# GpSimd instead of VectorE makes the low parts of 14 weight tiles in the first block of a three-block layer kernel

## The chip, the core and the metric

The kernel runs on one core of a Trainium2 chip. The metric is the device time of one execution in microseconds (us). Three executions of the kernel before took 2788.99, 2790.64 and 2792.49 us; the median is 2790.64 us.

The engines are named as the profile names them: PE is TensorE, DVE is VectorE, ACT is ScalarE, POOL is GpSimd, SP is SyncE, which here issues the weight loads.

## The reference, cut to what matters

Three blocks follow each other on a sequence of 256 positions of width 1024, all in float32. The change lies in the middle of the first block, between its first feed-forward part and its memory attention:

```python
h = x @ w_in
g_ssd, g_att, z, xbc, dt_raw, q, c_kv, q_idx, k_idx, w_idx = split_cols(h, IN_SPLITS)
y_ssd = ssd_branch(z, xbc, dt_raw, ...)          # a scan over the sequence, then a gated norm
# dsa_branch: an index score picks 64 of 256 keys for each query, then attention over them
q_lat = einsum('bthd,hdr->bthr', q, w_uk)
score = where(causal, sum over heads of relu(q_idx @ k_idx) * w_idx, -inf)
_, idx = lax.top_k(score, topk)
y_att = softmax(q_lat @ c_kv[idx] - slope * dist) @ c_kv[idx], then @ w_uv
merged = sigmoid(g_ssd) * (y_ssd @ w_proj_ssd) + sigmoid(g_att) * (y_att @ w_proj_att)
x = layer_norm(ALPHA * x + merged @ w_out)
```

The kernel makes keys from `c_kv @ w_uk` and values from `c_kv @ w_uv` and does the attention as an ordinary masked one.

## The kernel before

Every matrix product is done with float32 precision from operands that TensorE takes in a reduced form (`fp32r`). A weight tile of up to 128 x 2048 elements is loaded into a buffer `raw`. ScalarE copies it, rounded, to `hi` (line 693); another engine then computes `lo = raw - hi` in place of `raw` (line 696). For each product TensorE issues three matmuls, lines 714 to 716: high by high, high by low, low by high.

The list `SEQ` fixes the order of all weight tiles. Outside the expert part of block two there are six `raw` buffers and three `hi` buffers, used in turn, so tile n can be rounded once TensorE has used tile n-3. `split_tile` is called for each tile by ScalarE (rounds) and by VectorE (subtracts), at the point of each engine's program that `refill` sets: after the step that belongs to tile n-3. For the tiles in the list `POOLED`, VectorE skips the call and GpSimd does the subtraction, at a place in GpSimd's program that is written out by hand. In the kernel before these are two tiles each of `misc`, `rva` and `sva` and the two tiles that follow the experts.

Each engine runs its instructions in order. A wait on a semaphore holds up everything that is queued behind it on that engine.

In the stage of the change (`tiles1`, with the side work of `pe_side1`, `act_side1`, `dve_side1` woven in, one side step after each tile) the tiles come in this order: `qi` 4, `ki` 1, `z` 4, `gs` 4, `q` 4, `uk` 1, `uv` 1, `ps` 4, `ga` 4; `pa` 4 follow. The 14 tiles from `q` to `ga` are the ones that the change moves. On VectorE the side work under these tiles is, in this order:

- the gated norm of the scan: line 1592, eight instructions in a row, `Yt = Yt * rs * nrow`, both tensors in SBUF;
- the index scores: line 1657 (`LG`, from PSUM), a reduction (line 1663), and the additions into `sc` (lines 1666 and 1669, both operands in SBUF);
- the search for the 64 largest (lines 1676, 1678), the mask made from it (line 1682 with one tensor operand, line 1684 with two in SBUF);
- eight attention steps: per step four times line 1704 (`bt` from `kd` and `MA`, both in SBUF), twice line 1707 (`SS` from PSUM and `bt`), the row maximum (line 1208), its negation (line 1210, 128x4), then of the step before the scaled output (line 1244, from PSUM) and the transposed scores (line 1234, from PSUM). Line 1608 drains the `ps` product from PSUM.

In the loop of `tiles1` VectorE does its part for a tile in the order: evictions, one side step, `refill` (the `lo` of the next tile), one more side step. GpSimd has nothing to do in this stage but to wait, after the loads of `drow`, `mraw`, `nrow` and `kd` at 213 to 215 us, for the start of the transposes of the attention's output (`o1`, 503 us), when it loads `mem` into the same buffer.

Of the kernel before, what the change touches and what calls it, by code (L numbers as in the profile page):

```python
# [79 lines left out]
def sequence():  # L80
    s = seq_ffn([("f1u", "f1d")], FF // P)
    s += seq_tm("misc", 8, 288, 288) + seq_fm("xbc", 8, 2048, 256)
    s += seq_fm("qi", 8, D, 256) + seq_fm("ki", 8, 128, 128) + seq_tm("z", 8, D, 512) + seq_tm("gs", 8, D, 512)
    s += seq_fm("q", 8, D, 256) + seq_fm("uk", 2, D, D) + seq_tm("uv", 2, D, D)
    s += seq_tm("ps", 8, D, 512) + seq_tm("ga", 8, D, 512) + seq_tm("pa", 8, D, D)
    s += seq_tm("mva", 8, 512, 512) + seq_tm("wo", 8, D, D)
    s += seq_fm("mk", 8, D, 256) + seq_fm("mq", 8, D, 256) + seq_tm("mvb", 8, 512, 512) + seq_tm("mo", 8, D, D)
    s += seq_ffn([("f2u", "f2d")], FF // P)
    s += seq_tm("rva", 8, 512, 512) + seq_fm("rqk", 8, 2048, 256) + seq_tm("rvb", 8, 1536, 512)
    s += seq_tm("rg", 8, 2048, 512)  # L90
    s += seq_tm("ro", 16, D, D)
    s += seq_ffn([("f3u", "f3d")], FF // P)
    s += seq_tm("sva", 8, 512, 512) + seq_fm("sk", 8, D, 256) + seq_fm("sq", 8, D, 256)
    s += seq_tm("svb", 8, 512, 512) + seq_tm("so", 8, D, D)
    s += seq_fm("rt", 8, P, P)
    s += seq_experts()
    for name in ("t1", "t2", "t4", "t5", "t3"):
        s += seq_tm(name, 8, 512, 512)
    s += seq_fm("gb", 8, P, P) + seq_fm("cf", 8, 512, 256)
    s += seq_tm("c1k", 16, 256, 256) + seq_tm("c1v", 16, 256, 256) + seq_tm("za", 8, 512, 512)  # L100
    s += seq_tm("gma", 8, D, 512) + seq_tm("ba", 4, D, 512) + seq_tm("zb", 8, 512, 512)
    s += seq_tm("gmb", 8, D, 512) + seq_tm("bb", 4, D, 512) + seq_tm("o3", 8, D, D)
    return s
# [144 lines left out]
SEQ = sequence()  # L248
OFFS = np.cumsum([0] + [P * nc_ * k for _, _, nc_, _, k in SEQ])
E0 = min(n for n, q in enumerate(SEQ) if q[0] == "e0u")  # L250
E1 = 1 + max(n for n, q in enumerate(SEQ) if q[0] == f"e{NE - 1}d")

POOLED = [n for name in ("misc", "rva", "sva") for n, q in enumerate(SEQ) if q[0] == name] + [E1, E1 + 1]
A1 = 2.0 ** 0.25
A2 = 4.0 ** 0.25

# [1 line left out]
def cells(n):  # L258
    return SEQ[n][2] * SEQ[n][4]
# [163 lines left out]
def program(nc, d, out):  # L423
    ctx = ExitStack()
    with ctx:
# [3 lines left out]
        def sb(c, name, shape, dt=F32):  # L429
            return c.take(name, shape, dt)  # L430
# [12 lines left out]
        def f32(ap):  # L443
            return ap.bitcast(F32)
# [63 lines left out]
        misc = sb(one_, "misc", [P, 2, 288])  # L508
# [160 lines left out]
        book, ps = Book(), {}  # L669
# [11 lines left out]
        def split_tile(L, n):  # L681

            if L.kind == "V" and n in POOLED:
                return
            slot, before, _ = HI_AT[L.path]
            m = cells(n)
            hi = HI[slot[n]][:, 0:m]
            raw, lo = [x[:, 0:m] for x in RAW[RAW_AT[L.path][0][n]]]
            if L.kind == "A":
                if before[n] is not None:  # L690
                    L.wait_ge("used", before[n])
                L.wait_ge("raw", n)
                L.e.activation(hi, raw, ACT.Copy).then_inc(*L.up("hi", n))  # L693
            else:
                L.wait_ge("hi", n)
                L.e.tensor_tensor(lo, raw, f32(hi), ALU.subtract).then_inc(*L.up("lo", n))  # L696
# [259 lines left out]
        def pool_gb(G, j, *after):  # L956
            for point in after:
                G.wait_ge(*point)
            src = d["rows"][j * 2 * D:(j + 1) * 2 * D].partition_broadcast(P)
            G.e.dma_start(GB[:, :, :].rearrange("p a n -> p (a n)"), src).then_inc(  # L960
                *G.landed(sem_ld["gb"], 16 * (j + 1), "lnw", j))

        def small_load(G, name, dst, src):
            G.e.dma_start(dst, src).then_inc(*G.landed(sem_ld[name], 16, name))

        def row_src(o, n):
            return d["rows"][o:o + n].partition_broadcast(P)
# [1234 lines left out]
        def met(L, name):  # L2202
            for kind in "TAV":
                L.wait_ge(name, kind)

        def branch(L, few, many):

            if L.kind in "TAV":
                meet(L, "moe")
            else:  # L2210
                met(L, "moe")
            v = L.e.value_load(flag[0:1, 0:1], min_val=0, max_val=1)
            seen, at = L.seen, L.next
            with L.e.If(v == 0):
                L.path, L.seen = "z", dict(seen)
                few(L)
            with L.e.Else():
                L.path, L.seen, L.next = "o", dict(seen), at
                many(L)
            L.path, L.seen = None, seen  # L2220
# [994 lines left out]
            run(ev_tm(V, "o3", 8, D, D, ev_o3))  # L3215

        def pool_end(G):
            for n in POOLED[6:8]:
                split_tile(G, n)
            G.wait_ge("norm", 7, 1)  # L3220
            G.wait_ge("scr")
            for tt in range(2):
                n = P * (tt + 1)
                src = bass.AP(d["scr"].tensor, T - 1 - tt * P, [[384, P], [P * 385, 16], [1, n]])
                small_load(G, f"bi{tt}", BI[:, :, tt * P:tt * P + n], src)
            small_load(G, "cm", cm_[:, :, :, :].rearrange("p a t c -> p (a t c)"), d["c_cmpm"])
            small_load(G, "w2", W2[:, :, :, :].rearrange("p a b n -> p (a b n)"), d["w2c"])
# [211 lines left out]
        def gpsimd(G):  # L3439
            G.wait_ge("raw", 0)  # L3440
            small_load(G, "cols", cols[:, :], d["cols"])
            pool_gb(G, 0, ("raw", 2))
            for n in POOLED[0:2]:
                split_tile(G, n)
            pool_gb(G, 1, ("norm", 0, 1))
            met(G, "f1")
            small_load(G, "drow", drow[:, :], row_src(16 * D, 48))
            small_load(G, "mraw", mraw[:, :], d["c_mneg4"])
            small_load(G, "nrow", nrow[:, :], row_src(16 * D + 48, D))
            small_load(G, "kd", kd[:, :, :, :].rearrange("p a t k -> p (a t k)"), d["c_dsa"])  # L3450
            G.wait_ge("o1", 6)
            small_load(G, "mem", M[:, :, :], d["mem"].rearrange("a (t p) n -> p (a t) n", p=P))
            pool_gb(G, 2, ("norm", 1, 1))
            pool_gb(G, 3, ("norm", 2, 1))
            for n in POOLED[2:4]:
                split_tile(G, n)
            pool_gb(G, 4, ("norm", 3, 1))
            met(G, "f2")
            small_load(G, "rope", rope[:, :, :].rearrange("p a t -> p (a t)"), d["c_rope"])
            small_load(G, "decay", DT[:, :, :, :].rearrange("p m h t -> p (m h t)"), d["c_decay"])  # L3460
            pool_gb(G, 5, ("norm", 4, 1))
            met(G, "ro")
            small_load(G, "hot", hot[:, :], d["c_hot"])
            small_load(G, "hneg", hneg[:, :], d["c_hneg"])
            small_load(G, "rel", rb[:, :], d["rel"])
            G.wait_ge("ev", ("dist",))
            src = dr[:, 0:384].unsqueeze(1).to_broadcast([16, P, 384])
            small_load(G, "scr", bass.AP(d["scr"].tensor, 0, [[P * 385, 16], [385, P], [1, 384]]), src)
            for n in POOLED[4:6]:
                split_tile(G, n)  # L3470
            pool_gb(G, 6, ("norm", 5, 1))
            met(G, "f3")
            small_load(G, "cs", cs[:, :, :].rearrange("p a n -> p (a n)"), d["c_sb"])
            pool_gb(G, 7, ("norm", 6, 1))
            met(G, "so")
            small_load(G, "nrow3", nrow3[:, :], row_src(17 * D + 48, D))
            branch(G, pool_end, pool_end)

        def sync(S):
# [3 lines left out]
            for n in range(E0 + RAWS):  # L3483
                load_tile(S, n)
            branch(S, sync_end, sync_end)

        kinds = (("T", "pe", tensor), ("A", "act", scalar), ("V", "dve", vector), ("G", "pool", gpsimd),
                 ("S", "sp", sync))
        sems = {k: {None: sem(f"s_{n}"), "z": sem(f"s_{n}_z"), "o": sem(f"s_{n}_o")} for k, n, _ in kinds}
# [44 lines left out]
```

## Time and profile before

| what | value |
| --- | --- |
| median of 3 executions | 2790.64 us |
| the profiled execution's own time | 2788.26 us |
| its span (first to last instruction) | 2786.1 us |
| PE busy in the span | 2639.0 us (95%) |
| DVE busy | 1946.9 us (70%) |
| ACT busy | 1528.6 us (55%) |
| POOL busy | 50.7 us (2%), 8 subtractions and DMA issues |
| line 696 on DVE, all of the kernel | 574 instructions, 1311.1 us |
| mean granted TensorE clock | 0.972 |

Times within the span are counted from its start. A row of the timeline gives the start, the time taken, engine, line, operation, output and inputs with their shapes, how many equal instructions were merged into it, and in brackets how long the engine had stood idle before it and what ended that. Most of the kernel is bound by TensorE; the stage from 365 to 505 us is one of the few in which TensorE stands idle several times.

### The profile page before, as it was taken

To read this page: it belongs to the slowest core of one execution; us is meant where nothing else is said; L and a number is where in the kernel's file an instruction comes from. 1 tells how busy PE (TensorE), PEld (TensorE's weight loads), DVE (VectorE), ACT (ScalarE), POOL (GpSimd) and SP (SyncE) were. 2 spreads that over 40 slices of the span, in tenths; PEclk is the share of its full clock that TensorE was granted. 3 is DMA by queue.
4 is the path that set the end of the run, shared out by engine and by line. 5 is a ranking of instruction groups with operands and counts; after the bars stand their busy time and mean duration, and the time that the engine had idled before them with its cause. 6 is when DMAs were issued, how large, how long until landed. Compare 5 with 4: busy or idle time off the path is not lost.

```text
span 2786.1 us, 34409 instructions
## 1 busy us (share of the span) xinstructions
PE 2639.0 (95%) x14799; PEld 2281.5 (82%) x14799; DVE 1946.9 (70%) x1940; ACT 1528.6 (55%) x1602; POOL 50.7 (2%) x38
## 2 busy tenths in 40 slices
PE   8999989998999998999878999999999999979998
PEld 7999877796998877998766888888888888867886
DVE  4457689565556665445547898988989898976854
ACT  4436445443444353434536777777777777755742
POOL 0000000000001000001000000000000000010000
PEclk9999999998999999999878999999999999989999
DMA  6545333452555534585227999999999999965332
GB/s 249 191 173 185 133 121 122 166 196 92 185 192 202 181 136 168 183 225 191 93 84 277 346 358 347 359 341 341 359 346 358 345 357 348 359 243 191 137 121 77
DMA packets 88640, 632.28 MB, mean 227 GB/s; under 512 B 9792, under 2 KB 9808, under 8 KB 13472
## 3 DMA queue, kind: packets, MB, share of 16 engines
q1 hardware_dynamic: 84496, 610.24, 59.7%
q0 software_dynamic: 3984, 19.76, 2.6%
q8 instruction: 118, 1.93, 0.3%
q14 instruction: 42, 0.34, 0.0%
HBM read 625.77 MB, written 4.19 MB: 226 GB/s over the span
## 4 chain that ended last, share of the span: by engine, by line
PE 85%; DVE 10%; ACT 3%; DMA 1%; issue 1%; DVEq 0%; POOL 0%; SPq 0%; ACTq 0%; POOLq 0%
PE pw L714 14%; PE pw L715 14%; PE pw L716 14%; PE py L714 12%; PE py L715 11%; PE py L716 11%; DVE lo L696 3%; ACT hi L693 1%; DMA raw<-in_wts 1%; PE pw L2404 1%; DVE XL L908 1%; PE pw L2341 1%; PE pw L870 1%; PE pw L2342 1%; PE pw L895 1%
## 5 line engine op out<-in xcount | busy, mean ns | idle before, releaser
L696 DVE TENSOR_TENSOR lo<-raw,hi 128x2048 fp32r<-128x2048 f32 x406 | 926.1, 2282 | 406.0 <-ACT hi L693 405.7
L693 ACT ACTIVATE hi<-raw 128x2048 fp32r<-128x2048 f32 x414 | 786.0, 1900 | 411.2 <-PE py L716 327.0
L714 PE MATMUL pw<-XH,hi 128*128 128x256 f32 x1688 | 484.0, 287 | 14.6 <-DVE lo L696 5.1
L715 PE MATMUL pw<-XL,hi 128*128 128x256 f32 x1688 | 481.9, 285 | 0.0
L716 PE MATMUL pw<-XH,lo 128*128 128x256 f32 x1688 | 481.7, 285 | 0.0
L696 DVE TENSOR_TENSOR lo<-raw,hix 128x2048 fp32r<-128x2048 f32 x168 | 385.0, 2292 | 53.5 <-ACT hix L693 49.6
L715 PE MATMUL pw<-lo,GH 128*128 128x512 f32 x896 | 354.2, 395 | 0.0
L714 PEld LDWEIGHTS pw<-XH,hi 128*128 128x128 f32 x1688 | 328.4, 195 | 19.9 <-DVE lo L696 6.1
L693 ACT ACTIVATE hix<-raw 128x2048 fp32r<-128x2048 f32 x168 | 321.7, 1916 | 39.2 <-PE py L716 37.6
L715 PEld LDWEIGHTS pw<-XL,hi 128*128 128x128 f32 x1688 | 328.4, 195 | 1.1
L716 PEld LDWEIGHTS pw<-XH,lo 128*128 128x128 f32 x1688 | 328.3, 194 | 0.0
L715 PE MATMUL py<-lo,hh 128*128 128x512 f32 x712 | 279.8, 393 | 0.0
L714 PE MATMUL py<-hi,XH 128*128 128x512 f32 (+1 forms) x480 | 195.5, 407 | 16.6 <-DVE XL L908 14.8
L715 PEld LDWEIGHTS pw<-lo,GH 128*128 128x128 f32 x896 | 169.3, 189 | 34.7
L714 PE MATMUL py<-hi,hh 128*128 128x512 f32 x484 | 190.7, 394 | 0.9 <-DVE hl L1110 0.5
L716 PE MATMUL py<-hi,XL 128*128 128x512 f32 (+1 forms) x480 | 190.2, 396 | 0.0
L715 PE MATMUL py<-lo,XH 128*128 128x512 f32 (+1 forms) x480 | 189.9, 396 | 0.0
L716 PE MATMUL py<-hi,hl 128*128 128x512 f32 x484 | 189.8, 392 | 0.0
L714 PE MATMUL pw<-hi,GH 128*128 128x512 f32 x452 | 184.5, 408 | 2.5 <-issue 2.5
L716 PE MATMUL pw<-hi,GL 128*128 128x512 f32 x452 | 179.7, 398 | 0.0
L714 PE MATMUL pw<-hix,GH 128*128 128x512 f32 x444 | 178.4, 402 | 0.0
L716 PE MATMUL pw<-hix,GL 128*128 128x512 f32 x444 | 174.6, 393 | 0.0
(509 smaller groups left out, 3840.0 us busy)
## 6 DMA issues: line engine op xcount, KB each, us to landing
raw<-in_wts SPq DMA_DIRECT2D x577, 1024.0 KB, 4.8
GB<-in_rows POOLq DMA_DIRECT2D x8, 1024.0 KB, 4.9
scratch_bias<-dr POOLq DMA_DIRECT2D x1, 3072.0 KB, 36.0
BI<-scratch_bias POOLq DMA_DIRECT2D x1, 2048.0 KB, 12.0
raw<-in_wts SPq DMA_DIRECT2D x3, 512.0 KB, 3.2
raw<-in_wts SPq DMA_DIRECT2D x2, 576.0 KB, 3.6
X<-in_x SPq DMA_DIRECT2D x1, 1024.0 KB, 5.4
nrow<-in_rows POOLq DMA_DIRECT2D x2, 512.0 KB, 4.6
```

The lines of the kernel that those rows point to most:

```text
L693: L.e.activation(hi, raw, ACT.Copy).then_inc(*L.up("hi", n))
L696: L.e.tensor_tensor(lo, raw, f32(hi), ALU.subtract).then_inc(*L.up("lo", n))
L714: T_.e.matmul(o, x[0], w[0], start=first, stop=False)
L715: T_.e.matmul(o, x[0], w[1], start=False, stop=False)
L716: return T_.e.matmul(o, x[1], w[0], start=False, stop=last)
L870: e = T_.e.transpose(o, src(tt, f0 + f), ident)
L895: e = T_.e.transpose(b[:, f * P:f * P + P], src[:, tt, (f0 + f) * P:(f0 + f + 1) * P], ident)
L908: V.e.tensor_tensor(lo[:, f0:f0 + 4, tt * P:tt * P + P], ps[key, tt, f0][:, :].rearrange("p (f t) -> p f t", f=4), f32(hi[:, f0:f0 + 4, tt ...
L2341: T_.e.matmul(b[:, f * P:f * P + P], TH[:, tt, fs], SL[:, tt, :], start=tt == 0, stop=False)
L2342: q = T_.e.matmul(b[:, f * P:f * P + P], TL[:, tt, fs], SL[:, tt, :], start=False, stop=tt == 1)
L2404: q = T_.e.transpose(bt_[:, g * P:g * P + P], ghf[(i - 1) % 2][:, g, :], ident)
```

## The change

`POOLED` gets the 14 tiles of `q`, `uk`, `uv`, `ps` and `ga`. So VectorE skips their subtraction, and GpSimd does all 14 in a row, after the load of `kd` and before it waits for `o1`. ScalarE's rounding, the loads, the buffers and TensorE's program stay as they are. The other edits only name the earlier pooled tiles in another way.

```diff
-POOLED = [n for name in ("misc", "rva", "sva") for n, q in enumerate(SEQ) if q[0] == name] + [E1, E1 + 1]
+def tiles_of(*names):
+    return [n for n, q in enumerate(SEQ) if q[0] in names]
+
+
+POOLED = tiles_of("misc", "q", "uk", "uv", "ps", "ga", "rva", "sva") + [E1, E1 + 1]
...
             small_load(G, "nrow", nrow[:, :], row_src(16 * D + 48, D))
             small_load(G, "kd", kd[:, :, :, :].rearrange("p a t k -> p (a t k)"), d["c_dsa"])
+            for n in tiles_of("q", "uk", "uv", "ps", "ga"):
+                split_tile(G, n)
             G.wait_ge("o1", 6)
             small_load(G, "mem", M[:, :, :], d["mem"].rearrange("a (t p) n -> p (a t) n", p=P))
```

Line numbers of the changed file are four higher here (696 is 700 there). GpSimd's program around the new place, before:

```order
L964 DMA kd<-in_c_dsa 128x1536
L964 DMA O<-in_mem 128x2x1024
L960 DMA GB<-in_rows 128x2048 x2
L696 TENSOR_TENSOR lo<-raw,hi 128x2048 x2
L960 DMA GB<-in_rows 128x2048
```

and after:

```order
L968 DMA kd<-in_c_dsa 128x1536
L700 TENSOR_TENSOR lo<-raw,hi 128x2048 x14
L968 DMA O<-in_mem 128x2x1024
L964 DMA GB<-in_rows 128x2048 x2
L700 TENSOR_TENSOR lo<-raw,hi 128x2048 x2
```

Fourteen subtractions now stand ahead of the load of `mem` into the buffer `O`.

VectorE's program at the index scores and the search for the largest, before (`sc` holds the scores, `m` the eight largest found):

```order
L854 COPY C<-pw 128x512
L1657 TENSOR_SCALAR LG<-pw,wi 128x256 x4
L1663 TENSOR_REDUCE sc<-LG 128x256
L1669 TENSOR_TENSOR sc<-sc,kd 128x256
L696 TENSOR_TENSOR lo<-raw,hi 128x2048
L1676 MAX m_144<-sc 128x8
L1678 MATCH_REPLACE sc<-m_144,sc 128x128
```

and after:

```order
L858 COPY C<-pw 128x512
L1661 TENSOR_SCALAR LG<-pw,wi 128x256 x4
L1667 TENSOR_REDUCE sc<-LG 128x256
L1673 TENSOR_TENSOR sc<-sc,kd 128x256
L1680 MAX m_144<-sc 128x8
L1682 MATCH_REPLACE sc<-m_144,sc 128x128
```

The subtraction between the scores and the search is gone; nothing else moved.

VectorE's program between two attention steps, before:

```order
L1208 TENSOR_REDUCE mx<-SS 128x4
L1210 TENSOR_SCALAR mx<-mx 128x4
L696 TENSOR_TENSOR lo<-raw,hi 128x2048
L1244 TENSOR_TENSOR O<-py,sm 128x256
L1268 RECIPROCAL sm<-sm 128x4
L1704 SCALAR_TENSOR_TENSOR bt<-kd,MA 128x256 x2
L1707 SCALAR_TENSOR_TENSOR SS<-pw,bt 128x2x256
```

and after:

```order
L1212 TENSOR_REDUCE mx<-SS 128x4
L1214 TENSOR_SCALAR mx<-mx 128x4
L1248 TENSOR_TENSOR O<-py,sm 128x256
L1272 RECIPROCAL sm<-sm 128x4
L1708 SCALAR_TENSOR_TENSOR bt<-kd,MA 128x256 x2
L1711 SCALAR_TENSOR_TENSOR SS<-pw,bt 128x2x256
```

The two-operand `bt` instructions now follow the maximum of the step before without the subtraction in between.

## Rows read from the trace of the kernel before

**Rows 1.** Busy time by stretch: length, PE, PEld, DVE, ACT, POOL, granted clock, DMA.

```profile
385.00:480.00 95.00, 85.11 (x506) 71.34 (x507) 87.93 (x170) 40.48 (x74) 0.00 (x0) 0.95 0.34 116
400.00:450.00 50.00, 41.98 (x235) 34.52 (x235) 47.09 (x99) 20.29 (x38) 0.00 (x0) 0.93 0.31 106
```

**Rows 2.** Waits from 365 to 510 us: waiter, releaser, total us, times, longest.

```profile
PE pw L1646 <- DVE C L854: 5.0, 1, 5.0
...
PE py L714 <- DVE MG L1608: 4.1, 2, 2.2
```

**Rows 3.** Chain that ended last, 385 to 480 us: shares by line, one piece.

```profile
by line: DVE lo L696 18.7%; DVE sc L1678 7.2%; DVE LG L1657 7.0%; DVE MA L1663 6.4%; DVE m L1676 6.3%; PE py L714 6.1%; PE py L716 5.5%; PE py L715 5.4%; DVE bt L1704 5.4%; DVE SS L1707 4.7%; DVE mx L1208 4.2%; issue 3.2%; PE py L1170 2.7%;
...
450.90 2.20 DVE lo L696
```

**Rows 4.** Timeline of POOL: four of its rows of subtractions.

```profile
195.05 2.66 POOL L696 TENSOR_TENSOR lo<-raw,hi 128x1152 fp32r<-128x1152 f32 x1 [179.98 <-ACT hi L693]
202.05 3.71 POOL L696 TENSOR_TENSOR lo<-raw,hi 128x1152 fp32r<-128x1152 f32 x1 [4.34 <-ACT hi L693]
...
863.76 4.62 POOL L696 TENSOR_TENSOR lo<-raw,hi 128x2048 fp32r<-128x2048 f32 x1 [184.10 <-ACT hi L693]
...
2489.26 9.02 POOL L696 TENSOR_TENSOR lo<-raw,hi 128x2048 fp32r<-128x2048 f32 x2 [1030.34 <-ACT hi L693]
```

**Rows 5.** Timeline of DVE beside those subtractions.

```profile
201.99 1.28 DVE L944 SCALAR_TENSOR_TENSOR X<-X,rs,GB 128x1024 f32<-128x1024 f32 x1
...
2493.33 1.42 DVE L930 BATCH_NORM_STATS2 st<-ACC 128x6 f32<-128x512 f32 x2
...
2495.10 4.26 DVE L937 SCALAR_TENSOR_TENSOR X<-ACC,mv,GB 128x1024 f32<-128x1024 f32 x1
```

**Rows 6.** Timeline of DVE at the scan's gated norm.

```profile
363.24 3.25 DVE L1592 SCALAR_TENSOR_TENSOR Yt<-Yt,rs,nrow 128x256 f32<-128x256 f32 x8
366.42 2.28 DVE L696 TENSOR_TENSOR lo<-raw,hi 128x2048 fp32r<-128x2048 f32 x1
368.74 0.87 DVE L1657 TENSOR_SCALAR LG<-pw,wi 128x128 f32<-128x128 f32 x3
```

**Rows 7.** Timeline of PE just behind it, and of DVE ten us later.

```profile
369.40 0.39 PE L714 MATMUL pw<-XH,hi 128*128 128x256 f32 x1 [2.70 <-DVE LG L1657]
...
379.87 1.29 DVE L884 TENSOR_TENSOR Y<-pw,Y 128x512 fp32r<-128x512 f32 x2 [3.76 <-ACT Y L877]
```

**Rows 8.** Timeline of ACT: four of the 14 tiles' roundings.

```profile
362.32 1.90 ACT L693 ACTIVATE hi<-raw 128x2048 fp32r<-128x2048 f32 x1
...
366.51 1.91 ACT L693 ACTIVATE hi<-raw 128x2048 fp32r<-128x2048 f32 x1
...
449.03 1.91 ACT L693 ACTIVATE hi<-raw 128x2048 fp32r<-128x2048 f32 x1 [6.79 <-PE py L716]
...
457.20 1.91 ACT L693 ACTIVATE hi<-raw 128x2048 fp32r<-128x2048 f32 x1 [4.23 <-PE py L716]
```

**Rows 9.** Timeline of DVE between two attention steps.

```profile
450.80 2.29 DVE L696 TENSOR_TENSOR lo<-raw,hi 128x2048 fp32r<-128x2048 f32 x1
...
454.00 0.76 DVE L1704 SCALAR_TENSOR_TENSOR bt<-kd,MA 128x256 f32<-128x256 f32 x2
...
458.37 0.17 DVE L1210 TENSOR_SCALAR mx<-mx 128x4 f32<-128x4 f32 x1
```

**Rows 10.** Timeline of DVE at the mask of the larger half.

```profile
444.52 0.29 DVE L1682 TENSOR_SCALAR sc<-sc 128x256 f32<-128x256 f32 x1
444.85 0.42 DVE L1684 TENSOR_TENSOR MA<-sc,kd 128x256 f32<-128x256 f32 x1
```

**Rows 11.** Busy time by stretch behind two idle times of PE, columns as in Rows 1.

```profile
366.40:369.80 3.40, 0.70 (x8) 0.51 (x6) 3.36 (x6) 2.02 (x2) 0.00 (x0) 0.98 0.85 308
369.80:373.20 3.40, 3.40 (x18) 3.40 (x18) 3.33 (x4) 0.00 (x0) 0.00 (x0) 0.51 0.00 0
407.00:414.00 7.00, 5.15 (x18) 4.32 (x19) 6.79 (x13) 0.19 (x1) 0.00 (x0) 0.52 0.00 0
```

More of the change, by code:

```diff
@@ L3217, in pool_end @@
         def pool_end(G):
-            for n in POOLED[6:8]:
+            for n in (E1, E1 + 1):
                 split_tile(G, n)
@@ L3442, in gpsimd @@
             pool_gb(G, 0, ("raw", 2))
-            for n in POOLED[0:2]:
+            for n in tiles_of("misc"):
                 split_tile(G, n)
@@ L3454, in gpsimd @@
             pool_gb(G, 3, ("norm", 2, 1))
-            for n in POOLED[2:4]:
+            for n in tiles_of("rva"):
                 split_tile(G, n)
@@ L3468, in gpsimd @@
             small_load(G, "scr", bass.AP(d["scr"].tensor, 0, [[P * 385, 16], [385, P], [1, 384]]), src)
-            for n in POOLED[4:6]:
+            for n in tiles_of("sva"):
                 split_tile(G, n)
```

## The prediction, made before the changed kernel was run

> **What bounds the kernel now.** I read the page first, then the busy time by stretch, the waits and the chain between 365 and 510 us, then the timelines of VectorE, ScalarE, GpSimd and TensorE there. Over the whole span TensorE is busy 95%, so only a stage in which it stands still can give time back. The stage of the 14 tiles is one. From 385 to 480 us TensorE is idle 95.0 - 85.1 = 9.9 us, VectorE is busy 87.9 of 95 us, and GpSimd does nothing [rows 1]. TensorE's longest waits there are for VectorE's drains of PSUM (5.0 us for `C`, 4.1 us for `MG`) [rows 2]. The chain that ended last goes through VectorE for most of this stretch, and its largest line is the subtraction that is to move: 18.7%, 2.20 us for one [rows 3]. So on VectorE, here, the subtraction is on the path. The change takes it off. The question is what GpSimd's fourteen passes cost VectorE in return.
>
> **What a pass on GpSimd does to VectorE.** An undisturbed pass over 128x2048 took 4.62 us, one over 128x1152 took 2.66 us [rows 4]. It is slower than VectorE's 2.28 us, but a `lo` is needed only after TensorE has gone through the two tiles before it, so the pass alone delays nobody. Two places of the trace show more. At 2495.10 VectorE's line 937, which subtracts and multiplies two SBUF tensors, took 4.26 us; line 944, of the same shape and kind, took 1.28 us at 201.99 [rows 5]. GpSimd's two passes lay from 2489.26 to 2498.28 [rows 4]. 2495.10 + 4.26 - 1.28 = 2498.08: the instruction did nothing until the pass was 0.2 us from its end, and then took its usual time. The statistics at 2493.33, with one SBUF operand, ran in the same pass at 0.71 us each, undelayed [rows 5]. The other way round, the pass that began at 202.05 took 3.71 us instead of 2.66, that is 1.05 us more, and line 944 still had 1.2 us to run when it began [rows 4, 5]. So a pass and a VectorE instruction with two SBUF operands exclude each other; the later one waits for the whole of the other. One clear case stands for the first direction and one for the second.
>
> **The change part by part.**
>
> *Removed.* Fourteen subtractions leave VectorE: 2.2 us of path each where VectorE is on the path [rows 3], ten of them (`uk`, `uv`, `ps`, `ga`) in the stretch of [rows 1]: 22 us.
>
> *Added: the first tiles (`q`).* The second tile's rounding ends at 362.32 + 1.90 = 364.2 us [rows 8]. GpSimd starts at once, and VectorE is then in line 1592, eight two-operand instructions of 0.41 us that began at 363.24 [rows 6]. If whoever has waited goes next, the pass starts behind the third (364.5) and lasts 4.62 - 0.17 = 4.45 us, to 368.95 (0.17 us is what the 3.71 us pass saved after line 944's end: 205.76 - 203.27 = 2.49 against 2.66). The next tile is rounded at 368.4 [rows 8], so after one more instruction of line 1592 the next pass runs, from 369.2 to 373.65. The other four end at 375.1; the first two `LG` take 0.6 us, and TensorE goes on at 375.7 instead of 369.40 [rows 7]: +6.3 us, with the removed subtraction of 366.42 already counted. Nothing behind it takes that up: VectorE stands idle 3.76 us at 379.87 because it waits, through ScalarE, for TensorE [rows 7]. If VectorE keeps its turn through all eight, `LG` starts 2.2 us earlier than now: -2.2 us. If GpSimd gets only the first pass in between, it is about +2.1. I take +6.3: in the rows the waiting instruction started when the running one ended, in both directions. No row shows a waiter while the other engine has a further two-operand instruction ready.
>
> *Added: the other ten passes.* I laid each pass at the end of its tile's rounding and looked for the first two-operand VectorE row in it. Two in full. The second `ga` tile is rounded at 450.94 [rows 8]; the pass lasts to 455.6. Without the subtraction of 450.80 the `bt` pair of 454.00 [rows 9] comes at 451.8 and waits until 455.4: 3.6 us lost for 2.2 won. The third is rounded at 459.11 [rows 8]; the pass lasts to 463.8. The negation of 458.37 (line 1210) [rows 9] comes 1.4 us late, at 459.8, and if it waits too, it waits 3.8 us. Done in the same way for all ten, in the tiles' order: 1.9, 0.1 (`uk`, `uv`), 2.9, 0.8, 3.9, 4.0 (`ps`), 1.4, 3.6, 3.8, 4.0 (`ga`), together 26.4 us. VectorE comes out 26.4 - 22 = +4.4 us longer. The bounds: no wait at all, and then the gain is limited by TensorE's idle 9.9 us [rows 1]; every pass met at its very start, 10 x 4.4 - 22 = +22 us. The value is worked from the timeline, so I hold it nearer than either.
>
> One price in it is not shown: whether instructions with a single SBUF operand wait. The statistics did not [rows 5]. But line 1682, one operand, takes 0.29 us for 256 elements where line 1684, two operands, takes 0.42 us [rows 10], so it reads its one operand at more than the usual rate. Line 1210 is of the same kind. If neither waits, the attention steps lose some 3.5 us less and the sum is +0.9; I take the waiting, for line 1682 resembles the two-operand row more than the statistics.
> The Trainium skill ("SBUF — State Buffer", section Who interferes with whom) says that VectorE's `tensor_scalar` in a two-port mode contends with GpSimd as well, and that `tensor_reduce` does not; no run here shows the first. By it the term is +4.4, without it +0.9.
>
> *TensorE's clock.* Behind the 2.7 us idle time before 369.40 the granted clock was 0.51 (1.2 GHz of 2.4) for 3.4 us. Behind the 5.0 us idle time at `C` [rows 2] it was 0.52 for 7 us [rows 11]. An idle time of 9 us before the third `q` product should draw at least the longer stretch: 3.6 us more at half clock, in which half of the work is lost, +1.8 us. Bounds 0 and about +4 (if another of the idle times draws one too).
>
> *At no cost.* `mem` is loaded behind the 14 passes now, but it waits for `o1` at 503 us, and the last pass ends some 30 us before. The four GpSimd loads ahead of the passes go out at 213 to 215 us as before. Loads on SP wait for TensorE's use of a tile, and follow it.
>
> **The sum.** 6.3 + 4.4 + 1.8 = +12.5 us. The profiled execution took 2788.26 us, 2.4 us under the median of 2790.64; on its own time the sum gives 2800.8, on the median 2803.1 us. I give the latter.
>
> **The rivals.**
>
> *VectorE keeps its turn (no change).* In line 1592 each instruction starts before the last has drained (eight of 0.48 us in 3.25 us) [rows 6], so GpSimd may never find a gap. Then -2.2 instead of +6.3, and no longer idle time: -2.2 + 4.4 = +2.2, 2792.8 us. For it: the overlap. Against it: in both directions the waiter started right at the end.
> The Trainium skill (same page, section SBUF: two separate sides) says that whichever starts first gets the pair of ports for the whole instruction and the other blocks; by that, a pass that asks before the next instruction is issued goes first, which is the forecast and not this rival. The trace agrees for single meetings (4.26 us, 3.71 us).
>
> *The exclusion hardly bites (faster).* If the 4.26 us had another cause, VectorE is 22 us shorter where it bounds, and TensorE gets back its idle time: 9.9 us [rows 1] and the 2.7 us before 369.40 [rows 7]: -12.6 us, 2778.0 us. It decides as soon as the ten waits together are under 22 us by more than 6. Against it stand two meetings that fit to 0.2 us.
>
> *Only two-operand instructions wait, with the handover as forecast.* 6.3 + 0.9 + 1.8 = +9.0, 2799.6 us; it is inside the forecast's range.
>
> **How the numbers follow.** A measurement of this kernel can tell about 0.2% (5.6 us) from no change. The forecast case, with the smaller price of the third rival in it, has 0.62, from 2797 to 2809 us; VectorE keeping its turn 0.26, 2788 to 2798; the exclusion that hardly bites 0.08; worse than 2809 (more idle time and half clock than I laid out) 0.04. Slower by over 0.2%: nearly all of the forecast (0.60), a fifth of the second case (0.05), the worse one (0.04): 0.69. Same: 0.02 + 0.19 + 0.01 = 0.22. Faster: 0.07 + 0.02 = 0.09. The range leaves out the faster rival, the lowest edge of the second and the worst: 2789 to 2809.
>
> **What would show it.** GpSimd busy some 67 us more, with passes of 4.4 to 4.9 us. In VectorE's timeline two-operand rows of 2 to 5 us: line 1592 twice over 4 us, line 1704 near 4 us in four or five attention steps, lines 1669 and 1684 or 1682 of 1 to 3 us; line 1707 and the reductions as before. TensorE idle about 9 us before the first `q` product. If line 1592 shows its 3.25 us unbroken, the second case holds; if no two-operand row is over 1.5 us, the third. The prediction is wrong above all if the handover in line 1592 goes the other way, or if ScalarE's rounding moves so that the passes meet other rows.

## The result and the profile after

The changed kernel took 2805.58 us (median of 5 executions, 2804.42 to 2805.76) against 2790.64 us in the comparison with it: a ratio of 1.0055, 95% interval 1.0041 to 1.007, or +15 us with an interval of +11 to +20. The forecast was 2803.1 us, slower, with a range from 2789 to 2809. The profiled execution took 2805.76 us (before: 2788.26), its span is 2804.0 us and the mean granted clock 0.968 (before 0.972). Line numbers are four higher than before.

Busy time of the engines over the whole span (us, share, instructions):

```profile
PE 2644.6 (94%) x14799; PEld 2286.7 (82%) x14799; DVE 1953.6 (70%) x1926; ACT 1528.5 (55%) x1602; POOL 114.9 (4%) x52
```

POOL is busy 114.9 - 50.7 = 64.2 us more. DVE has lost 14 subtractions and is busy 6.7 us *more*: a waiting instruction counts as busy. Line 1704, now 1708, and its like have swallowed what the subtractions gave up.

GpSimd's passes, from POOL's timeline (start, duration, operation, count, idle time before):

```profile
362.91 9.25 POOL L700 TENSOR_TENSOR lo<-raw,hi 128x2048 fp32r<-128x2048 f32 x2 [3.86 <-ACT hi L697]
...
413.07 4.50 POOL L700 TENSOR_TENSOR lo<-raw,hi 128x2048 fp32r<-128x2048 f32 x1 [1.90 <-ACT hi L697]
...
436.09 4.62 POOL L700 TENSOR_TENSOR lo<-raw,hi 128x2048 fp32r<-128x2048 f32 x1 [0.48 <-ACT hi L697]
446.00 4.60 POOL L700 TENSOR_TENSOR lo<-raw,hi 128x2048 fp32r<-128x2048 f32 x1 [5.29 <-ACT hi L697]
...
473.97 4.50 POOL L700 TENSOR_TENSOR lo<-raw,hi 128x2048 fp32r<-128x2048 f32 x1 [3.56 <-ACT hi L697]
```

DVE's timeline beside them:

```profile
361.85 11.78 DVE L1596 SCALAR_TENSOR_TENSOR Yt<-Yt,rs,nrow 128x256 f32<-128x256 f32 x8
...
401.98 1.98 DVE L1673 TENSOR_TENSOR sc<-sc,kd 128x256 f32<-128x256 f32 x1
...
414.36 3.30 DVE L1686 TENSOR_SCALAR sc<-sc 128x128 f32<-128x128 f32 x1
...
436.52 4.53 DVE L1708 SCALAR_TENSOR_TENSOR bt<-kd,MA 128x128 f32<-128x128 f32 x2
441.09 0.42 DVE L1711 SCALAR_TENSOR_TENSOR SS<-pw,bt 128x256 f32<-128x256 f32 x1
...
445.86 4.89 DVE L1708 SCALAR_TENSOR_TENSOR bt<-kd,MA 128x128 f32<-128x128 f32 x2
...
473.37 1.22 DVE L1212 TENSOR_REDUCE mx<-SS 128x4 f32<-128x1024 f32 x1
474.63 3.86 DVE L1214 TENSOR_SCALAR mx<-mx 128x4 f32<-128x4 f32 x1
```

Read the two lists against each other. The pair of line 1708 at 436.52 ends at 441.05: GpSimd's pass ends at 436.09 + 4.62 = 440.71, and one half of the pair follows. Line 1214, a negation of 4 columns, starts at 474.63 inside the pass from 473.97 to 478.47 and ends at 478.49. Line 1686 ends at 417.66, the pass beside it at 417.57. The reduction of line 1212 at 473.37 runs into the same pass as line 1214 and keeps its 1.22 us. The eight instructions at 361.85 took 3.25 us before [rows 6]; taken one by one, the fourth and the fifth took 4.76 and 4.71 us. TensorE waited for them:

```profile
374.33 0.58 PE L718 MATMUL pw<-XH,hi 128*128 128x256 f32 x1 [9.02 <-DVE LG L1661]
```

The chain that ended last, from 385 to 480 us (shares by line, then its longest pieces: start, length):

```profile
by line: DVE bt L1708 18.8%; PE pw L718 6.2%; DVE sc L1686 5.9%; PE pw L719 5.5%; PE pw L720 5.4%; PE pw L1650 5.3%; DVE sc L1682 5.1%; DVE mx L1214 4.8%; DVE SS L1711 4.7%; DVE m L1680 4.4%; DVE mx L1212 4.2%; PE py L718 4.1%; DVE LG L1661
...
436.52 4.54 DVE bt L1708 x2
445.86 4.90 DVE bt L1708 x2
466.59 4.44 DVE bt L1708 x2
474.63 3.86 DVE mx L1214
```

The subtraction's 18.7% of the chain [rows 3] is gone, and line 1708, 5.4% before, stands at 18.8%.

Busy time by stretch, columns as in [rows 1], and TensorE's longest waits from 385 to 480 us (waiter, releaser, total, times, longest):

```profile
385.00:480.00 95.00, 76.62 (x442) 65.14 (x443) 80.92 (x141) 33.30 (x62) 45.78 (x10) 0.87 0.31 109
400.00:450.00 50.00, 41.13 (x243) 35.06 (x242) 45.36 (x80) 18.16 (x30) 26.03 (x6) 0.86 0.31 114
```

```profile
PE py L718 <- DVE MG L1612: 7.8, 2, 4.8
...
PE pw L1650 <- DVE C L858: 5.7, 1, 5.7
```

TensorE is idle 95.0 - 76.62 = 18.4 us where it was idle 9.9 [rows 1], and its granted clock is 0.87 in place of 0.95.

### The profile page after: what moved, and what is told of

It reads as the page before. It is cut to its first block, busy times and chain, and to the rows that moved or that the text cites. A ratio compares the mean times of both kernels' runs of the same rounds, so it can differ in the third digit from the quotient of the medians.

```text
span 2804.0 us, 34417 instructions
## 1 busy us (share of the span) xinstructions
PE 2644.6 (94%) x14799; PEld 2286.7 (82%) x14799; DVE 1953.6 (70%) x1926; ACT 1528.5 (55%) x1602; POOL 114.9 (4%) x52
## 4 chain that ended last, share of the span: by engine, by line
PE 85%; DVE 10%; ACT 3%; DMA 1%; issue 1%; ACTq 0%; DVEq 0%; POOL 0%; SPq 0%; POOLq 0%
PE pw L718 14%; PE pw L719 14%; PE pw L720 14%; PE py L718 12%; PE py L719 11%; PE py L720 11%; DVE lo L700 2%; ACT hi L697 1%; DMA raw<-in_wts 1%; PE pw L2408 1%; DVE XL L912 1%; DVE bt L1708 1%; PE pw L2345 1%; PE pw L874 1%; PE pw L2346 1%
## 5 line engine op out<-in xcount | busy, mean ns | idle before, releaser
L700 DVE TENSOR_TENSOR lo<-raw,hi 128x2048 fp32r<-128x2048 f32 x392 | 893.9, 2282 | 406.2 <-ACT hi L697 406.1
```

## One stretch cut the same way in every kernel

To compare kernels I cut each trace at the same two instructions: the first of the sixteen 64x128 matmuls of the index scores before the first `q` product, and the first matmul with `YH` behind the stage. Between them lie 753 or 754 matmuls in each kernel. Busy time by stretch, of the kernel before:

```profile
365.44:504.61 139.17, 121.22 (x753) 103.88 (x752) 120.38 (x215) 62.55 (x112) 0.70 (x1) 0.95 0.33 114
```

and of the changed kernel:

```profile
364.05:522.54 158.49, 127.50 (x754) 109.67 (x753) 127.53 (x204) 62.55 (x112) 59.23 (x14) 0.88 0.29 100
```

The stretch is 19.3 us longer (it begins 1.4 us earlier and ends 17.9 us later). Of that, 30.99 - 17.95 = 13.0 us is idle time of TensorE and 127.50 - 121.22 = 6.3 us is the same matmuls run slower. Two numbers thus describe a kernel here: TensorE's idle time and its busy time. The table has both for all kernels of the study, with the time of the norm's eight instructions (line 1592 of before) and TensorE's idle time just before the first `q` product, each from the same rows of its trace.

| kernel | norm, us | idle before `q` | stretch | PE busy | PE idle | median us | ratio to before, 95% |
| --- | --- | --- | --- | --- | --- | --- | --- |
| before | 3.25 | 2.70 | 139.17 | 121.22 | 17.95 | 2790.64 | |
| changed | 11.78 | 9.02 | 158.49 | 127.50 | 30.99 | 2805.58 | 1.0055 [1.0041, 1.007] |
| e1_q_only | 11.78 | 9.01 | 145.60 | 123.25 | 22.35 | 2797.97 | 1.0028 [1.0015, 1.0041] |
| e2_no_q | 3.25 | 2.70 | 151.95 | 127.27 | 24.68 | 2801.05 | 1.0045 [1.0029, 1.0061] |
| e3_two_q | 11.78 | 9.02 | 145.26 | 121.03 | 24.23 | 2795.90 | 1.0026 [1.0015, 1.0037] |
| e4_quarters | 8.33 | 5.57 | 138.65 | 120.10 | 18.55 | 2785.60 | 0.999 [0.998, 1.0] |
| e5_after_norm | 3.25 | 0.50 | 147.51 | 125.03 | 22.48 | 2795.29 | 1.002 [1.0011, 1.0029] |
| e6_eighths | 5.62 | 2.87 | 130.39 | 117.15 | 13.24 | 2780.03 | 0.9974 [0.9964, 0.9985] |
| e8_memset | 3.25 | 0.50 | 122.92 | 115.47 | 7.45 | 2773.49 | 0.9945 [0.9932, 0.9959] |
| e9_quarters_norm | 3.25 | 0.50 | 133.36 | 121.61 | 11.75 | 2781.90 | 0.9976 [0.9967, 0.9986] |
| e10_eighths_norm | 3.25 | 0.49 | 129.50 | 118.63 | 10.87 | 2778.78 | 0.997 [0.9959, 0.998] |
| e11_memset_x3 | 3.25 | 0.50 | 124.18 | 117.01 | 7.17 | 2774.47 | 0.995 [0.9938, 0.9963] |
| e12_sixteenths | 4.47 | 2.05 | 135.31 | 119.92 | 15.39 | 2780.06 | 0.9971 [0.9959, 0.9984] |

Each comparison had its own executions of the kernel before, with medians from 2789.4 to 2790.6 us. A stretch comes from one profiled execution and a median from several, so they differ by a few us (most in `e4_quarters`: its profiled execution took 2793.50 us, 8 us over the median).

## The experiments

The theory was that a GpSimd pass over a tile and a VectorE instruction that needs two SBUF operands exclude each other. The main rival was that GpSimd's pass is only slower (4.6 us for 2.3), so that the low parts come late.

**Which tiles cost.** Three kernels give GpSimd only some of the tiles. In each, only the list changes (`e3_two_q` takes `tiles_of("q")[1:3]`, `e2_no_q` the other ten):

```diff
+GIVEN = tiles_of("q")
-POOLED = tiles_of("misc", "q", "uk", "uv", "ps", "ga", "rva", "sva") + [E1, E1 + 1]
+POOLED = tiles_of("misc", "rva", "sva") + GIVEN + [E1, E1 + 1]
...
-            for n in tiles_of("q", "uk", "uv", "ps", "ga"):
+            for n in GIVEN:
                 split_tile(G, n)
```

> Only the four q tiles go to GpSimd; uk, uv, ps and ga stay with VectorE. Theory (a GpSimd pass and a two-operand VectorE instruction exclude each other): the eight instructions of line 1592 still take about 11.8 us, TensorE still idles about 9 us before the first q product, later rows are as in the kernel before; the part of the shift that the changed kernel shows at the q product, +9.2 us, with a little more for half clock behind the long idle time: 2797 to 2803 us. Rival (GpSimd's pass is only slower, 4.6 us for 2.2, and nobody excludes anybody): the four low parts come 2.4 us later each, line 1592 at 3.25 us, at most +2.4 us: 2788 to 2793 us.

> Only the ten tiles of uk, uv, ps and ga go to GpSimd; q stays with VectorE. Theory: line 1592 takes 3.25 us again, the attention steps show their two-operand rows of 4 to 5 us, and the shift is what the changed kernel lost between the q product and 488 us, +8.7 us (the prediction's sum had +4.4 there): 2795 to 2801 us. Rival (pass only slower): ten subtractions fewer on VectorE where it bounds, so TensorE gets idle time back: 2778 to 2788 us.

> Only the second and third q tile go to GpSimd. Theory: these two passes are the ones that get in between line 1592's instructions, so they alone make the series about 11.8 us long and leave TensorE idle about 9 us before the first q product: the same time as with all four q tiles, within 1.5 us, 2797 to 2803 us. Rival (each pass costs its own lateness): half of what four q tiles cost.

DVE and PE of `e3_two_q` around the norm:

```profile
363.93 11.78 DVE L1597 SCALAR_TENSOR_TENSOR Yt<-Yt,rs,nrow 128x256 f32<-128x256 f32 x8
```

```profile
376.41 0.58 PE L719 MATMUL pw<-XH,hi 128*128 128x256 f32 x1 [9.02 <-DVE LG L1662]
```

The same two rows of `e2_no_q`:

```profile
362.19 3.25 DVE L1597 SCALAR_TENSOR_TENSOR Yt<-Yt,rs,nrow 128x256 f32<-128x256 f32 x8
```

```profile
368.35 0.58 PE L719 MATMUL pw<-XH,hi 128*128 128x256 f32 x1 [2.70 <-DVE LG L1662]
```

Two passes are enough to make the norm 8.5 us longer, and the wait of TensorE is for VectorE's drain `LG`, not for a low part. The four `q` tiles cost 8.3 us (interval 4 to 11), two of them 6.2 us (`e3_two_q`, 1 us under the lowest that was expected; its interval, 4 to 10 us, overlaps with that of `e1_q_only`). The ten other tiles cost 11.4 us, the upper edge of what was expected; there the rival had a gain of 3 to 13 us and is out. The two groups add up to 20 us against 15 for the whole change, which the intervals allow.

**Take the collision away, keep the passes.** In `e5_after_norm` the passes stay whole and the second one waits for the norm's end:

```diff
             for n in tiles_of("q", "uk", "uv", "ps", "ga"):
+                if n == tiles_of("q")[1]:
+                    G.wait_ge("ssd", "y")
                 split_tile(G, n)
```

> All 14 tiles on GpSimd in whole passes, but the second pass waits until line 1592's eight instructions are done. Theory (exclusion, the waiter goes next): the series takes 3.25 us again, TensorE's 9 us before the first q product shrink to under 3 us, and what is left is the price of the ten other tiles alone, which e2_no_q gave as +11.4 us: 2796 to 2803 us. Rival (the q tiles cost because GpSimd's passes are slow and come late): the low parts come later still, TensorE waits longer for them, the time stays at or above the changed kernel's: 2805 to 2812 us.

It took 2795.29 us, 10 us less than the changed kernel and 0.7 us under the lowest that was expected, though three low parts now come later. The rival wanted 2805 or more. TensorE waits 0.50 us before the first `q` product, less than the 2.70 of before, since the subtraction that stood between the norm and `LG` [rows 6] is no longer VectorE's.

**Same work in shorter pieces.** `e4_quarters`, `e6_eighths` and `e12_sixteenths` cut each of the 14 subtractions by columns, into k = 4, 8 and 16 (`GIVEN` holds all 14 tiles here). Only the last piece releases the low part, so no low part comes earlier by it:

```diff
-                L.e.tensor_tensor(lo, raw, f32(hi), ALU.subtract).then_inc(*L.up("lo", n))
+                k = 4 if n in GIVEN else 1
+                for p in range(k):
+                    c = slice(p * m // k, (p + 1) * m // k)
+                    L.e.tensor_tensor(lo[:, c], raw[:, c], f32(hi)[:, c], ALU.subtract).then_inc(
+                        *(L.up("lo", n) if p == k - 1 else L.up()))
```

> All 14 tiles on GpSimd, each in four instructions over 512 columns (some 1.2 us each) in place of one. Theory: whoever waits goes next, so a two-operand VectorE instruction waits for one quarter (up to 1.2 us) and no longer for a whole pass (up to 4.6 us). The ten meetings of the attention steps then cost 12 us at most against 22 us won, line 1592 still loses some 4 us: no row of line 1708 over 2 us, and the kernel takes 2779 to 2788 us, so it may beat the kernel before. Rival (slower pass, or contention for memory spread over all instructions): four pieces take as long as one pass or longer, 2804 us or more.

> As e4_quarters, but each of the 14 tiles in eight instructions over 256 columns (some 0.6 us each). Theory: a meeting costs at most 0.6 us, half of what it cost with quarters; line 1592's eight instructions take at most 8 x (0.4 + 0.6) = 8 us, no row of line 1708 is over 1.2 us, and the kernel is 1 to 6 us faster than e4_quarters: 2778 to 2785 us. Rival (the gain of the quarters came from finer starts of the low parts, not from shorter meetings): no further gain, 2785 us or more, since each piece adds its fixed cost on GpSimd.

> As e6_eighths, in sixteen instructions over 128 columns for each of the 14 tiles. Theory: a meeting costs at most about 0.4 us, but each instruction adds its fixed cost on GpSimd (a tile took 4.6 us whole, about 4.9 in quarters, 5.9 in eighths), so a tile takes 7 to 8 us and the low parts begin to come late: within 3 us of e6_eighths, 2777 to 2783 us. If only the length of a meeting counted: another 2 to 4 us faster, 2775 to 2778 us.

POOL's groups of subtractions in `e6_eighths` (busy us, mean ns of one, idle time before):

```profile
L704 POOL TENSOR_TENSOR lo<-raw,hi 128x256 fp32r<-128x256 f32 x112 | 82.7, 774 | 168.3 <-ACT hi L698 168.3
L704 POOL TENSOR_TENSOR lo<-raw,hi 128x2048 fp32r<-128x2048 f32 x6 | 28.0, 4676 | 1302.3 <-ACT hi L698 1302.3
```

A tile takes 8 x 0.774 = 6.2 us in place of 4.7 on GpSimd (waits included), a third more, and the kernel is 25 us faster than the changed one. So it isn't GpSimd's time that counts but how long VectorE is shut out at once. The longest pairs of line 1708 (here 1713) took 4.89 us with whole passes, 2.94 with quarters, 1.80 with eighths and 1.22 with sixteenths. Quarters:

```profile
467.11 2.94 DVE L1713 SCALAR_TENSOR_TENSOR bt<-kd,MA 128x256 f32<-128x256 f32 x2
```

Eighths:

```profile
445.44 1.80 DVE L1713 SCALAR_TENSOR_TENSOR bt<-kd,MA 128x256 f32<-128x256 f32 x2
```

Sixteenths:

```profile
452.43 1.22 DVE L1713 SCALAR_TENSOR_TENSOR bt<-kd,MA 128x256 f32<-128x256 f32 x2
```

My limits of 2 and 1.2 us for the first two were too low: a pair can meet two pieces. Quarters cannot be told from the kernel before; eighths are 0.26% faster. Sixteenths bring nothing on top, as the theory expected from GpSimd's fixed cost (16 x 0.480 = 7.7 us a tile), but the trace shows another reason. DVE and POOL in `e12_sixteenths`:

```profile
435.27 7.34 DVE L1691 TENSOR_SCALAR sc<-sc 128x256 f32<-128x256 f32 x1
```

```profile
429.51 12.95 POOL L704 TENSOR_TENSOR lo<-raw,hi 128x128 fp32r<-128x128 f32 x31
```

The one-operand line 1691 (0.29 us alone, [rows 10]) was not let in between two pieces. It waited until the row of 31 pieces ended at 442.46 us, and TensorE then stood idle 6.7 us for VectorE's `MG`.

**Both together.** `e9_quarters_norm` and `e10_eighths_norm` join the pieces with the wait of `e5_after_norm`:

> Quarters as in e4_quarters, and the second tile waits until line 1592's eight instructions are done. Theory: the series is whole (3.25 us), TensorE's 5.6 us of idle time before the first q product in e4_quarters become under 3 us, and less half clock behind them: 2 to 6 us faster than e4_quarters, 2779 to 2784 us, which beats the kernel before. Rival (the handover in the series is not what the quarters still lose): as e4_quarters, 2785 us, or slower because the third and fourth q tile come later.

> Eighths as in e6_eighths, and the second tile waits until line 1592's eight instructions are done. Theory: the series takes 3.25 us again; e6_eighths still lost 2.9 us of TensorE's idle time before the first q product there, and about as much should come back: 2776 to 2780 us. Rival (the wait makes GpSimd, whose eighths together take about 6 us a tile, late with the third and fourth q tile): the same as e6_eighths or slower, 2780 to 2784 us.

With quarters the medians differ by 4 us (2785.60 and 2781.90), as much as expected, and the idle time before `q` shrinks from 5.57 to 0.50 us; but the intervals of the two ratios just overlap, so the gain is likely and not shown. With eighths the norm is whole too and the idle time before `q` shrinks from 2.87 to 0.49 us, but the intervals for 2778.78 and 2780.03 us overlap widely: no difference that can be told. `e10_eighths_norm` beats both kernels of the case, by 0.2 to 0.4% the one before.

**Is it the reading?** In `e8_memset` GpSimd writes zeros over the 14 low parts instead of subtracting, so the products leave these low parts out; the edit below is its edit. `e11_memset_x3` writes them three times, and only the third write releases the tile.

```diff
+                if n in GIVEN:
+                    L.e.memset(f32(lo), 0.0).then_inc(*L.up("lo", n))
+                else:
+                    L.e.tensor_tensor(lo, raw, f32(hi), ALU.subtract).then_inc(*L.up("lo", n))
```

> GpSimd writes zeros over the 14 low parts instead of subtracting, so it reads nothing, and the low parts of these tiles are left out of the products. Theory as the Trainium skill words it ("SBUF - State Buffer", section SBUF: two separate sides: VectorE with two SBUF inputs blocks only against a GpSimd operation that reads SBUF): line 1592 takes 3.25 us, lines 1708 and 1673 about 0.7 us, single-operand lines such as 1686 and 1214 may still wait; the relief comes without its price, 2774 to 2784 us. Rival (any GpSimd instruction over the tile holds VectorE up): two-operand rows are held up as long as the writes last, 2795 us or more if a write pass lasts as long as a subtraction.

> As e8_memset (the low parts of the 14 tiles are zeros), but each tile is written three times, 3 x 1.81 = 5.4 us on GpSimd, longer than a subtraction's pass of 4.6 us, and only the third write releases the tile. Theory (what holds VectorE up is that GpSimd's subtraction reads the tile, not how long GpSimd is busy or how late the low part comes): two-operand rows stay undelayed, line 1592 at 3.25 us and line 1708 under 0.6 us, and the kernel stays near e8_memset: 2772 to 2778 us; single-operand lines such as 1686 and 1214 may wait for one write, up to 1.8 us each, and if they do it is up to 2782 us. Rival (a GpSimd pass of 5 us makes the low parts late for TensorE, or holds up everything): 2790 us or more.

DVE in `e11_memset_x3`:

```profile
416.36 0.49 DVE L1715 SCALAR_TENSOR_TENSOR bt<-kd,MA 128x128 f32<-128x128 f32 x2
...
426.83 1.41 DVE L1221 TENSOR_SCALAR mx<-mx 128x4 f32<-128x4 f32 x1
...
432.22 1.18 DVE L1693 TENSOR_SCALAR sc<-sc 128x256 f32<-128x256 f32 x1
```

POOL at the same time:

```profile
412.44 11.03 POOL L705 MEMSET lo<- 128x2048 f32 x6 [5.84 <-ACT hi L698]
424.54 5.55 POOL L705 MEMSET lo<- 128x2048 f32 x3 [1.07 <-ACT hi L698]
431.44 5.58 POOL L705 MEMSET lo<- 128x2048 f32 x3 [1.35 <-ACT hi L698]
```

Three writes keep GpSimd busy for 5.5 us, longer than the subtraction's 4.6, and release the low part later. Still the kernel takes 2774.47 us, 31 us less than the changed one. The pair of line 1715 at 416.36 goes through in 0.49 us inside the six writes from 412.44 to 423.47, and the norm takes 3.25 us. That a write lasts only 1.8 us is not the reason: quarters last 1.34 us on average, and pairs beside them took up to 2.94. So lateness is not the cause, and a GpSimd instruction that reads nothing does not hold up two-operand VectorE instructions. The one-operand ones do wait, 1.41 us for a 128x4 that takes 0.17, at most for one write of 1.81 us.
The Trainium skill ("SBUF — State Buffer", section SBUF: two separate sides) has this distinction: two SBUF inputs contend only with a GpSimd operation that reads SBUF, a two-port mode with any. The two memset kernels agree on the first count (0.49 us). On the second they agree if lines 1221 and 1693 (1.41 and 1.18 us) run in such a mode, which no row states.
What the relief is worth without its price can be read here as well: 2773.49 us, 16 us under the kernel before and half a us under the lowest that was expected. The prediction's second rival had put it at 2778.0.

## Why the prediction was right, step by step

*What bounds the stage.* Right. Without contention (`e8_memset`) the fourteen subtractions taken off VectorE give 16 us back; TensorE's idle time in the stretch falls from 17.95 to 7.45 us and the time of its matmuls from 121.22 to 115.47. The second rival's 12.6 us counted idle time alone. (The 4.1 us that the prediction read for `MG` were two waits, the longer of 2.2 us [rows 2].)

*A pass and a two-operand instruction exclude each other.* Right, and shown: it was read from two meetings [rows 4, 5], and the traces of the changed kernel, of the pieces and of the memsets follow it.

*The `q` tiles, +6.3 us.* The handover went as taken: the waiting pass got in twice, behind the third and behind the fourth instruction. The forecast had the norm end at 375.1 us and TensorE go on at 375.7 after 9 us. The stage began 1.4 us earlier, the norm ended at 373.63, and the first `q` product started at 374.33 after 9.02 us. The first rival (VectorE keeps its turn) would have shown 3.25 us. `e3_two_q` shows that these two passes do it. `e1_q_only` ends the stretch 6.8 us later than before, and its median lies 8.3 us higher.

*Ten passes, 26.4 us of waiting against 22 won.* Measured, in the tiles' order, from rows like those above less the duration alone: 1.6, 0.4 (`uk`, `uv`), 3.1, 0.6, 4.0, 4.4 (`ps`), 2.0, 3.7, 3.7, 3.7 (`ga`), together 27.2 us where 1.9, 0.1, 2.9, 0.8, 3.9, 4.0, 1.4, 3.6, 3.8, 4.0 had been laid out. The smaller price of the third rival is out: lines 1686 and 1214 did wait, 3.30, 2.26 and 3.86 us.

*TensorE's clock, +1.8 us, bounds 0 and 4.* This term was mis-sized: the same matmuls took 6.3 us more, above its upper bound. The prediction counted one longer half-clock time behind the 9 us of idling and at most one more. The changed kernel has five rows at half clock in this stage:

```profile
370.30:380.50 10.20, 6.17 (x29) 6.17 (x30) 8.31 (x16) 0.00 (x0) 1.86 (x1) 0.50 0.00 0
387.40:394.20 6.80, 6.80 (x31) 6.58 (x31) 3.59 (x8) 0.05 (x1) 2.71 (x1) 0.50 0.01 2
414.70:424.90 10.20, 6.26 (x24) 5.43 (x25) 9.99 (x14) 0.60 (x1) 2.87 (x1) 0.50 0.05 18
445.40:448.80 3.40, 3.40 (x12) 2.63 (x9) 3.19 (x4) 2.54 (x10) 2.80 (x1) 0.50 0.00 0
476.10:482.90 6.80, 3.77 (x9) 3.00 (x10) 6.35 (x10) 2.07 (x8) 2.36 (x1) 0.50 0.01 4
```

That is 37.4 us, with 26.41 us of matmuls in it. Before, it was 13.6 us with 11.95:

```profile
369.70:373.10 3.40, 3.40 (x18) 3.40 (x17) 3.33 (x4) 0.00 (x0) 0.00 (x0) 0.50 0.00 0
407.20:414.00 6.80, 5.15 (x18) 4.32 (x19) 6.59 (x13) 0.19 (x1) 0.00 (x0) 0.50 0.00 0
461.80:465.20 3.40, 3.40 (x10) 2.61 (x9) 2.95 (x8) 0.00 (x0) 0.00 (x0) 0.51 0.00 0
```

Half of the difference, 7.2 us, is near the 6.3 us measured. The row behind the 9 us of idling, set against the first row of before, accounts for (6.17 - 3.40) / 2 = 1.4 us, near the term; the other four rows make the rest. `e2_no_q` has nearly the whole 6.3 us (127.27 - 121.22 = 6.05) although its norm is undisturbed, and `e3_two_q`, with the 9 us of idling and no pass behind it, has none of it (121.03). So most of it comes from the shorter idle times that the ten other passes make, with their own time at 1.2 in place of 2.4 GHz. The prediction sized the longest idle time and allowed for one more.

*The sum.* Terms of 6.3, 4.4 and 1.8 gave +12.5 us. Measured in the stretch: idle time +13.0 us (forecast 6.3 + 4.4 = 10.7), slower matmuls +6.3, less 1.4 us of earlier start: +17.9 at its end, +17.5 us in the profiled execution and +14.9 between the medians. Of the 5.4 us by which the stretch ends later than forecast, 4.5 are the clock's and 2.3 are idle time, less the 1.4 us of earlier start. Between the medians only 2.5 us are missing. The result lies in the range because the range had room above the sum; that the point came so near is in part luck, since the clock's term was too small by more than that.

*What would show it.* GpSimd was to be busy 67 us more (64.2), line 1592 to be broken twice (4.76 and 4.71 us, 11.78 in all), line 1704 to be near 4 us in four or five steps (4.53, 4.89 and 4.43 twice), lines 1669 and 1682 to take 1 to 3 us (2.61, 1.98; 3.30, 2.26), and line 1707 and the reductions to be as before (0.42 and 1.22 us). All hold but for the 3.30 us, a little over.

What stays open: why line 1691 was kept out of the 31 sixteenths for 7.34 us. At 430.91 us, in the same row of pieces, the one-operand line 1219 (1210 of before) took 0.39 us and so lost only 0.2 us, and two-operand lines got in between pieces elsewhere. Nor does the number of operands decide: at 383.58 us in the same kernel the two-operand line 1675, 0.29 us alone, took 1.71 us, and like line 1691 it ended 0.15 us behind the end of a row of pieces (48 of them, to 385.14 us). No run here tells these apart.

## What to carry to other kernels

Before work goes from VectorE to GpSimd, lay each GpSimd pass beside VectorE's timeline and look for the first instruction in it that has two SBUF operands, or a single one that it reads at more than the usual rate, as line 1682 does here [rows 10]. What it waits there is the price, and tile by tile it could be worked out here from the trace of the kernel before to some tenths of a us. If the price is too high, cut the pass into pieces: GpSimd then works longer in all and VectorE waits less (here up to eighths; sixteenths brought no more). And where waits are spread over a stage, count TensorE's time at half clock behind every idle time, not behind the longest one alone.

## What was not expected of the hardware

A 128x4 instruction with one operand waited for nearly a whole GpSimd pass (3.86 us for 0.17); the prediction had taken this into its sum, but no row had shown it. In a row of 31 short GpSimd subtractions without a gap such an instruction waited 7.34 us, so shorter pieces are not better without end. Writing 128x2048 zeros took GpSimd 1.81 us and held up no two-operand instruction.
